# Two-block kernel on one Trainium2 core: the mixing, feed-forward and final norms with squares read from PSUM, sums in four column tiles, roots on four token columns, part of the residual adds on GpSimd, and no barrier

## The reference

```python
mix = token_mixer(h_lat, w_in, w_out, ...)                # ends in a product with w_out
x = x + gt_a * rms_norm_2(mix, g_mix_post)                # norm "mx"
h_ffn = modulate(rms_norm_2(x, g_ffn_pre), sh_f, sc_f)    # norm "fp"
ffn = conv_ffn(h_ffn, w_up, conv_w, conv_b, w_down, rows)
x = x + gt_f * rms_norm_2(ffn, g_ffn_post)                # norm "fo", and the output

def rms_norm_2(x, g):
    xf = xf * lax.rsqrt(jnp.mean(xf * xf, axis=-1, keepdims=True) + NORM_EPS)
    return xf.astype(x.dtype) * g
```

## Time and profile before

| | |
|---|---|
| median of 3 runs | 2103.09 us (2102.45 to 2104.31) |
| profiled execution | 2099.98 us, span 2098.2 us |
| PE busy | 1995.7 us (95% of the span) |
| PEld busy | 1577.6 us (75%) |
| DVE busy | 1176.8 us (56%) |
| ACT busy | 782.9 us (37%) |
| POOL busy | 146.1 us (7%) |
| chain that ended last | PE 70%, issue 17%, DVE 7%, ACT 2%, POOL 2% |

### The profile page before, as it was taken

One profiled execution on the slowest core, in us unless ns is written; L12 is line 12 of the kernel. 1 busy time (PEld: TensorE's weight loads), 2 busy tenths in 40 slices (PEclk: granted clock), 3 DMA queues, 4 the chain that ended last, 5 costly groups with the idle time before them and its releaser, 6 DMA issues.

```text
span 2098.2 us, 34740 instructions
## 1 busy us (share of the span) xinstructions
PE 1995.7 (95%) x14160; PEld 1577.6 (75%) x14160; DVE 1176.8 (56%) x1777; ACT 782.9 (37%) x1361; POOL 146.1 (7%) x116
## 2 busy tenths in 40 slices
PE   7999999979999999999999999999999959999996
PEld 1577799968787877776777787877886738888884
DVE  5489766666544344467485746576563265556324
ACT  5786433334322222337532212235242224444211
POOL 0000132210202022000002202020000000000000
PEclk9999999989999999999999999999999979999998
DMA  5221000032233232220244453634520212232421
GB/s 186 103 91 51 1 4 4 9 138 91 91 102 99 90 97 83 92 92 31 94 167 141 141 180 130 210 122 162 153 89 10 71 69 92 96 100 84 151 80 40
DMA packets 60713, 201.37 MB, mean 96 GB/s; under 512 B 7968, under 2 KB 10912, under 8 KB 59296
## 3 DMA queue, kind: packets, MB, share of 16 engines
q1 hardware_dynamic: 59808, 192.86, 27.6%
q10 hardware_dynamic: 768, 6.55, 1.0%
HBM read 190.61 MB, written 6.42 MB: 94 GB/s over the span
## 4 chain that ended last, share of the span: by engine, by line
PE 70%; issue 17%; DVE 7%; ACT 2%; POOL 2%; SPq 1%; DMA 1%; DVEq 0%; ACTq 0%; POOLq 0%
PE bank L1868 17%; PE bank L1869 16%; PE bank L1870 16%; POOL HS L2559 2%; PE bank L2016 1%; PE bank L2038 1%; PE bank L2053 1%; PE bank L1863 1%; PE bank L2020 1%; DVE HR L1490 1%; DVE GBZ L1311 1%; PE bank L2299 1%; PE bank L2285 1%; PE bank L2320 1%; PE bank L2430 1%
## 5 line engine op out<-in xcount | busy, mean ns | idle before, releaser
L1161 DVE TENSOR_TENSOR wlo<-raw,whi 128x1024 fp32r<-128x1024 f32 x270 | 327.6, 1223 | 590.5 <-ACT whi L668 589.0
L668 ACT ACTIVATE whi<-raw 128x1024 fp32r<-128x1024 f32 x270 | 282.3, 1056 | 735.7 <-PE bank L1870 706.1
L1868 PE MATMUL bank<-inh,whi 128*128 128x512 f32 x1200 | 472.5, 394 | 19.4 <-DVEq L1803 16.1
L1869 PE MATMUL bank<-inl,whi 128*128 128x512 f32 x1200 | 468.9, 391 | 0.0
L1870 PE MATMUL bank<-inh,wlo 128*128 128x512 f32 x1200 | 468.7, 391 | 0.0
L1868 PEld LDWEIGHTS bank<-inh,whi 128*128 128x128 f32 x1200 | 226.5, 189 | 77.2 <-DVEq L1803 17.0
L1869 PEld LDWEIGHTS bank<-inl,whi 128*128 128x128 f32 x1200 | 226.6, 189 | 47.3 <-issue 1.0
L1870 PEld LDWEIGHTS bank<-inh,wlo 128*128 128x128 f32 x1200 | 226.4, 189 | 47.5
L1868 PE MATMUL bank<-hidh,whi 128*128 128x512 f32 x576 | 228.6, 397 | 14.7 <-DVE hidl L1466 8.1
L1870 PE MATMUL bank<-hidh,wlo 128*128 128x512 f32 x576 | 224.4, 390 | 0.0
L1869 PE MATMUL bank<-hidl,whi 128*128 128x512 f32 x576 | 224.4, 390 | 0.0
(11 more groups left out here) (361 smaller groups left out, 2769.8 us busy)
## 6 DMA issues: line engine op xcount, KB each, us to landing
raw<-in_mlp_w SPq DMA_DIRECT2D x128, 512.0 KB, 3.6
ADW<-in_w_ada SPq DMA_DIRECT2D x32, 768.0 KB, 4.8
raw<-in_w_up SPq DMA_DIRECT2D x44, 512.0 KB, 3.5
raw<-in_w_in SPq DMA_DIRECT2D x28, 512.0 KB, 3.6
raw<-in_a_w_rkv SPq DMA_DIRECT2D x24, 512.0 KB, 3.3
raw<-in_w_down SPq DMA_DIRECT2D x22, 512.0 KB, 3.5
raw<-in_a_wo SPq DMA_DIRECT2D x8, 512.0 KB, 8.3
raw<-in_b_wq SPq DMA_DIRECT2D x8, 512.0 KB, 3.2
```

What stands on the lines that cost most here:

```text
L668: act.activation(whi[u % SLOTS][:, :], raw[u % SLOTS][:, :], ACT.Copy).then_inc(w_hi, 1)
L1161: dve.tensor_tensor(lo[:, :], r[:, :], h[:, :].bitcast(F32), ALU.subtract).then_inc(w_lo, 1)
L1868: pe.matmul(o, w[:, wc], xh, start=start, stop=False)
L1869: pe.matmul(o, w[:, wc], xl_, start=False, stop=False)
```

## The change

1. ACT squares each block straight from its PSUM bank, for "mx" and "fo"; DVE's copy of a bank waits for its square.
2. The squares go into four tiles (SQ4). PE adds them in two rounds of four matmuls, each with 128x32 ones into its own 32 partitions. The first round stands between two products of the last weight unit: for "mx" after bank 5, for "fo" after bank 2. A square of the second round waits for the sum of the first that used its tile.
3. ACT copies the 128x512 of partial sums to SBUF (PARTS). PE multiplies its four pieces of 128 tokens with one column of ones, giving 128x4. ACT takes the root and DVE the reciprocal of 128x4 (RTOK), and PE spreads it over 128x512 in a bank, from which DVE reads it.
4. The additions of `add_normed`: GpSimd makes the first five in order, DVE the last three. Squares of "fp" and the stores at the end follow the order in which the additions are expected (ADDED).
5. The barrier is gone. PE waits before each of the eight blocks of up pass 0 for its low part alone. DVE waits for its own last low part before it goes on.
6. Before the squares of "fo" ACT takes one root of a single number, which loads the table there.

```diff
+        DOWN = (4, 5, 6, 7, 0, 1, 2, 3)
+        BY_POOL, ADDED = 5, (0, 1, 2, 5, 3, 6, 4, 7)
+        STAT_ORDER = {"mx": tuple(range(CB)), "fp": ADDED, "fo": DOWN}
...
-            for m in range(CB):
-                sp.wait_ge(STEP["dve_ffn"].sem, STEP["dve_ffn"].at(("out", m)))
+            for n in ADDED:
+                m, owner = DOWN[n], STEP["pool_ret" if n < BY_POOL else "dve_ffn"]
+                sp.wait_ge(owner.sem, owner.at(("out", m)))
                 sp.dma_start(out[:, m, :], X2[:, m, :]).then_inc(stored, 16)
...
-            stats_of("mx", lambda kb: MX[:, kb, :], lambda kb: act.wait_ge(drt.sem, drt.at(("mx", kb))))
-            stats_of("fp", lambda kb: X[:, kb, :], lambda kb: act.wait_ge(drt.sem, drt.at(("x", kb))))
+            def square_at(name, pos, block_):
+                kb = STAT_ORDER[name][pos]
+                if pos >= 4:
+                    act.wait_ge(pn.sem, pn.at(("sum", name, STAT_ORDER[name][pos - 4])))
+                act.activation(SQ4[pos % 4][:], block_, ACT.Square).then_inc(an.sem, an.step(("sq", name, kb)))
+            def token_root(name, bank, columns):
+                act.wait_ge(pn.sem, pn.at(("sum", name, STAT_ORDER[name][CB - 1])))
+                act.activation(PARTS[:], bank[:], ACT.Copy).then_inc(an.sem, an.step(("part", name)))
+                act.wait_ge(pn.sem, pn.at(("total", name)))
+                act.activation(RTOK[:, 0, :], columns[:, 0:TB], ACT.Sqrt, scale=1.0 / (32 * C), bias=small[:, 0:1]).then_inc(an.sem, an.step(("root", name)))
+            for m in range(CB):
+                act.wait_ge(lin.sem, lin.at(("bank", "mx", m)))
+                square_at("mx", m, PB[m][:])
+            token_root("mx", PB[0], PB[1])
...
-            act.drain().then_inc(phase, 1)
-            act.wait_ge(phase, phase_done("act"))
             act.wait_ge(spill, 32)
...
+            act.activation(small[:, 94:95], small[:, 0:1], ACT.Sqrt).then_inc(an.sem, an.step())
+            for pos, m in enumerate(DOWN):
+                act.wait_ge(lin.sem, lin.at(("bank", "down", m)))
+                square_at("fo", pos, PB[m][:])
+            token_root("fo", PB[4], PB[5])
...
             for m in range(CB):
-                dve.wait_ge(lin.sem, lin.at(("bank", "mx", m)))
+                dve.wait_ge(an.sem, an.at(("sq", "mx", m)))
                 dve.tensor_copy(MX[:, m, :], PB[m][:]).then_inc(drt.sem, drt.step(("mx", m)))
...
+            def add_normed(src, gain, bank, dst, blocks, steps, mark):
+                for n, kb in enumerate(blocks):
+                    dve.scalar_tensor_tensor(src[:, kb, :], src[:, kb, :], gain[:, kb:kb + 1], bank[:], ALU.mult, ALU.mult).then_inc(steps.sem, steps.step(("nx", mark, kb)))
+                    if n >= BY_POOL:
+                        dve.wait_ge(steps.sem, steps.at(("nx", mark, kb)))
+                        dve.tensor_tensor(dst[:, kb, :], dst[:, kb, :], src[:, kb, :], ALU.add).then_inc(steps.sem, steps.step((mark, kb)))
+            token_rstd("mx")
+            add_normed(MX, GP, PB[2], X, range(CB), drt, "x")
+            token_rstd("fp")
+            dve.wait_ge(STEP["pool_ret"].sem, STEP["pool_ret"].at(("x", BY_POOL - 1)))
+            modulated("fp", X, GF, TQ, inh, inl, lambda kb: adac[:, 24 + kb, 0:1], scale=PB[5])
             dve.wait_ge(spill, 32)
+            dve.wait_ge(dad.sem, dad.at(("lo", "fp", CB - 1)))
...
+            def sums_round(name, bank, first, free=None):
+                if free is not None:
+                    pe.wait_ge(free[0].sem, free[0].at(free[1]))
+                for pos in range(first, first + 4):
+                    kb, g = STAT_ORDER[name][pos], pos % 4
+                    pe.wait_ge(STEP["act_norm"].sem, STEP["act_norm"].at(("sq", name, kb)))
+                    pe.matmul(bank[32 * g:32 * g + 32, :], sq("ones")[:, 0:32], SQ4[g][:], start=pos < 4, stop=pos >= 4).then_inc(pn.sem, pn.step(("sum", name, kb)))
+            def token_scales(name, columns, bank, free):
+                pe.wait_ge(free[0].sem, free[0].at(free[1]))
+                pe.wait_ge(STEP["act_norm"].sem, STEP["act_norm"].at(("part", name)))
+                for tb in range(TB):
+                    mm = pe.matmul(columns[:, tb:tb + 1], PARTS[:, chunk(tb)], sq("ones")[:, 0:1], start=True, stop=True)
+                mm.then_inc(pn.sem, pn.step(("total", name)))
+                pe.wait_ge(STEP["dve_norm"].sem, STEP["dve_norm"].at(("rstd", name)))
+                for tb in range(TB):
+                    mm = pe.matmul(bank[:, chunk(tb)], RTOK[:, 1, tb:tb + 1].to_broadcast([P, P]), sq("ident"), start=True, stop=True)
+                mm.then_inc(pn.sem, pn.step(("spread", name)))
...
-            sums("mx")
-            sums("fp")
-            pe.drain().then_inc(phase, 1)
-            pe.wait_ge(phase, phase_done("pe"))
+            sums_round("mx", PB[0], 4)
+            token_scales("mx", PB[1], PB[2], (drt, ("mx", 7)))
+            sums_round("fp", PB[3], 0)
+            sums_round("fp", PB[3], 4)
+            token_scales("fp", PB[4], PB[5], (drt, ("mx", 7)))
...
+                            if m == 0 and s.freed is None:
+                                pe.wait_ge(dad.sem, dad.at(("lo", "fp", kb)))
...
+                    if k == NFB - 1 and m == 2:
+                        sums_round("fo", PB[4], 0, (dff, ("fo", 4)))
+            sums_round("fo", PB[4], 4)
+            token_scales("fo", PB[5], PB[6], (dff, ("fo", 7)))
...
+            def add_normed(src, dst, blocks, steps, mark):
+                for kb in blocks:
+                    pool.wait_ge(steps.sem, steps.at(("nx", mark, kb)))
+                    pool.tensor_tensor(dst[:, kb, :], dst[:, kb, :], src[:, kb, :], ALU.add).then_inc(prs.sem, prs.step((mark, kb)))
+            add_normed(MX, X, range(BY_POOL), STEP["dve_ret"], "x")
+            add_normed(FO, X2, DOWN[:BY_POOL], STEP["dve_ffn"], "out")
```

More of the change, by code:

```diff
@@ L408, in program @@
         RSQ = at("RSQ", 204, [T])
+        PARTS = at("PARTS", 204, [T])
+        RTOK = at("RTOK", 206.25, [2, TB])
         RN = at("RN", 206, [2, TB])
@@ L1013, in _ @@
             mlp(1, UM1, "mlp1", "bo", UBO + 7)
-            def stats_of(name, block_, ready=None, n=T):
-                for kb in range(CB):
-                    if ready is not None:
-                        ready(kb)
-                    if kb >= 2:
-                        act.wait_ge(pn.sem, pn.at(("sum", name, kb - 2)))
-                    act.activation(SQT[kb % 2][:, :n], block_(kb), ACT.Square).then_inc(an.sem, an.step(("sq", name, kb)))
-                act.wait_ge(pn.sem, pn.at(("sum", name, CB - 1)))
-                act.activation(RS[:, :n], PB[0][:, :n], ACT.Sqrt, scale=1.0 / C, bias=small[:, 0:1]).then_inc(an.sem, an.step(("root", name)))
             for kb in range(CB):
@@ L1801, in _, with token_rstd @@
-            add_normed(MX, GP, X, drt, "x")
-            modulated("fp", X, GF, TQ, inh, inl, lambda kb: adac[:, 24 + kb, 0:1])
-            dve.drain().then_inc(phase, 1)
-            dve.wait_ge(phase, phase_done("dve"))
+            def token_rstd(name):
+                dve.wait_ge(an.sem, an.at(("root", name)))
+                dve.reciprocal(RTOK[:, 1, :], RTOK[:, 0, :]).then_inc(dn.sem, dn.step(("rstd", name)))
+                dve.wait_ge(STEP["pe_norm"].sem, STEP["pe_norm"].at(("spread", name)))
@@ L1836, in _ @@
             split_run(UF + 44, NFB - 3)
[L1837 to L1838 removed]
+            for m in DOWN:
+                dve.wait_ge(an.sem, an.at(("sq", "fo", m)))
                 dve.tensor_copy(FO[:, m, :], PB[m][:]).then_inc(dff.sem, dff.step(("fo", m)))
[L1840 removed]
+            token_rstd("fo")
             dve.wait_ge(fill, 32)
[L1842 removed]
+            add_normed(FO, GFP, PB[6], X2, DOWN, dff, "out")
         @block.tensor
@@ L2508, in _ @@
                 pe.wait_ge(w_lo, UF + 44 + k + 1)
-                for m in order:
+                for m in DOWN:
                     if k == 0:
```

27 lines of the change are left out of this document (8 added, 19 removed).

## The result

The changed kernel took 2080.65 us (median of 4 runs, 2080.02 to 2084.11), the kernel before on the same chip 2103.7 us (4 runs, 2102.45 to 2104.38). The ratio is 0.9895 with an interval of 0.9883 to 0.9907. Forecast were 2079.5 us, in a range of 2075.5 to 2084.0.

A forecast was written before the change was run, and what follows sets the result against it. PE, busy in 95% of the span, was taken as the bound, so its standstills count. Gains of 17.31 us up to the first up product and 6.33 at the end, 23.6 in all, took 2103.09 to 2079.5 us, range 2075.5 to 2084.

The forecast's parts named there:

- The additions: After "mx" and "fo", first multiplication to end of last addition: 8.05 us; at the end a gain of 2.15 from 10.20.
- The barrier: Behind norm "fp", from modulation's start to the first up product: 2.34 us instead of 11.97, a gain of 9.63.
- The norm chain from the last square: From a norm's last square to DVE's first read of the spread: 4.80 us, summed from steps in the old trace.
- The place of the first round: After bank 5 in "mx", bank 2 in "fo": the round takes 1.06 us, and the second round's squares wait for it.
- The wait on the operation just issued: Each DVE addition waits for the multiplication right before it: 0.04 us taken for the wait; six waits of 0.12 in all.
- The clock: At the start of up pass 0 PE runs at about half clock; this slow start's cost of 2.8 us was kept.
- Two of the signs of being wrong: GpSimd additions over 1.5 us, and a granted clock of 0.5 between the sums of "fp".
- A: Rival: PE's clock also falls in "fp", 3 us more, 2082.5 us; chance 0.2.
- B: Rival: PE's clock is full when up pass 0 starts, 2.8 us less, 2076.7 us; chance 0.18.
- C: Rival: GpSimd's additions take 2.04 us each, 2 x 2.95 us later, 2085.4 us; chance 0.06.
- D: Rival: up pass 0's early start wins nothing, starved for its fourth weight unit or a missed wait; 2089 us, chance 0.04.
- E: Rival: slower than before, PE left at 1.2 GHz far into the up passes, 38 us for two, 2118 us; chance 0.02.

The follow-up runs named there:

- the second profile: The changed kernel run again unchanged, on the third chip: 2079.0 us, ratio 0.9889 to the kernel before.
- the last experiment but one: Against the changed kernel with eight square tiles and filler matmuls: DVE's three additions moved behind all eight multiplications; 2074.47 us.
- The fillers: Against the changed kernel: added matmuls of ones in PE's pauses at "mx" and "fp", into a bank nobody reads; 2076.94 us.

## Why the prediction was right, and where it was off

The mechanism held: 23.64 us were forecast, 22.85 found piece by piece, 23.05 between the medians. That the total is so near is in part luck. The additions (0.39 at each place), the clock in "mx" (0.52 over the forecast) and the barrier (0.09) fell short, while "fo" (0.46) and the chain of "fp" (0.14) came out better.

- **The barrier** (9.63 forecast) measured 9.54, and both experiments that moved it alone show it. That the split of the fourth unit and the save of X hide behind the products was right.
- **The norm chain from the last square** (4.80) measured 4.66 and 4.67 in "fp". Durations from the retention head carried over.
- **The place of the first round.** I counted four squares that wait for the whole round, last one done 3.55 after bank 5. It was 3.29 in "mx" (1677.39 - 1674.10) and 3.20 in "fo". That each square waits only for the sum of its own tile is not what won this: the first of them starts 1.14 after the round began, when the round (1.06) is over. The squares follow each other more closely than I had them, four in 2.15 and 2.06 where I had 2.44. That and the shorter chain (4.67 for 4.80) are why "fo" came out 0.46 better than forecast. What I did not see is that with eight tiles all of it could go.
- **"mx"** measured 8.87 where 8.35 was forecast, because the clock had fallen: the spread took 2.07 us instead of 1.16. In the second profile, at full clock, it is 7.95, 0.4 better than forecast.
- **The additions** are the term that was mis-sized: 8.46 and 8.44 for 8.05. The step that failed is "its first operations take 2.04/2 = 1.02 while DVE only multiplies with a bank", and the 1.47 behind it, taken from rows in which GpSimd squares one tile, `HS<-HR`. An addition of two different tiles takes 1.27, and 1.72 beside DVE's additions. GpSimd is through at 7.90 and not at 6.8, so it is still at work beside DVE's last addition, which takes 0.99 and not the 0.68 that I gave it. That is 0.31 of the 0.41; the rest is in the first two additions, 1.02 and 0.99 where I had 0.92, less 0.06 by which the first starts earlier. The mechanism, DVE last, was right by half a microsecond only (8.46 against 7.90); with six additions it turns.
- **The wait on the operation just issued**, 0.12 each: the trace has 1687.99 + 0.73 = 1688.72 to 1688.76, 0.04 as forecast. But the last experiment but one shows that this way of taking them away wins nothing, since what replaces them costs more.
- **The clock.** Keeping 2.8 us of slow start was right: 16 matmuls in 6.2 us again. The fillers show what it is worth, 2.5 us there (361.11 to 358.58).
- **Two of the signs of being wrong** did show: GpSimd additions over 1.5 us (1.72), and a granted clock of 0.50 between the first sums of "fp", until 1691. The first is the mis-sized term. The second cost nothing, since those sums wait for the additions; the last sums and the chain of "fp" had the full clock again (4.66).

The prediction also says that the trace does not show GpSimd's addition at this size. It does: in the kernel before, L2530 adds two different tiles and L2543 multiplies two, eight and forty times. Behind the bar stand the busy time of all in us and the mean of one in ns.

```profile
L2543 POOL TENSOR_TENSOR LM<-LL,sqs 128x512 f32<-128x512 f32 x40 | 50.1, 1273 | 62.7 <-PE bank L2038 62.4
L2530 POOL TENSOR_TENSOR GBZ<-GBZ,sqs 128x512 f32<-128x512 f32 x8 | 10.2, 1269 | 307.7 <-DVE GBZ L1300 307.7
```

So the 1.27 us could have been read ahead of the run, and the 0.25 us over the square go with the second input tile and not with the kind of operation: the square is a multiplication too.

The rivals. A put the low clock into "fp" at 3 us. The clock did fall ahead of the up passes, but in "mx", or in "fo", or (eight tiles) in "fp", and it costs 0.8 to 0.9 us for each spread that lies wholly in it, since of my three PE parts only the spread grew. With the barrier put back it met two. B came true only with work in PE's pauses, which the fillers are. C's price (2.04) was never seen; the highest is 1.72. D and E are excluded by the equal time from first product to bank 2, 361.11 us after and 361.19 before.

What stays open is what makes the clock fall in none, one or two of the chains, and the several microseconds by which executions differ ahead of 560 us. Whether a third product between the rounds would help four tiles was not tried.

## What to carry to other kernels

Where engines hand a chain of small steps to one another, price it from the same chain elsewhere in the trace, step by step; here it held within 0.15 us at full clock. For an operation of GpSimd take the duration of the same number of different input tiles, not merely of the same shape: the addition and the multiplication of two tiles take 1.27 alike, the square of one 1.02. And keep DVE's second tile in a bank while GpSimd works, which here was worth 4.1 us in eight blocks. Where an early step needs buffers to be freed, first ask whether there is room for more buffers: four more tiles were worth 1.1 and 1.6 us beyond the best order found with four.
